# Top-k attention started before the last strip's choice is finished, and the last gate tile of two attentions spread to their ends

## The reference, cut to what matters

```
# fox attention, 16 heads of 64: softmax over causal keys with a forget bias, then a gate
s = einsum(q, k) * scale + (c_q - c_k);  w = softmax(s);  attn = w @ v
y = (attn * silu(g)) @ w_out

# top-k attention, 8 heads of 64: the indexer scores every key, the 128 best are kept
isc = einsum(relu(q_i . k_i), w_i) * idx_scale      # [query, key], causal
_, sel = lax.top_k(isc, 128)                        # ties: lowest key first
p = softmax(q_a . k_a over sel);  oa = p @ v_a

# stick-breaking attention ob, then
merged = sigmoid(gate_a) * (oa @ w_up_a) + sigmoid(gate_b) * (ob @ w_up_b)
```

## Time and profile before

| | |
|---|---|
| median of 3 runs | 1633.67 us (1633.66 to 1635.63) |
| the profiled execution's own time | 1633.67 us |
| span from its first to its last instruction | 1631.9 us |
| mean granted PE clock | 0.993 of 2.4 GHz |
| PE busy | 1554.3 us, 95% of the span |
| DVE busy | 874.0 us, 54% |
| ACT busy | 633.2 us, 39% |
| POOL busy | 609.8 us, 37% |

### The profile page before, as it was taken

One profiled execution on the slowest core, in us unless ns is written; L12 is line 12 of the kernel. 1 busy time (PEld: TensorE's weight loads), 2 busy tenths in 40 slices (PEclk: granted clock), 3 DMA queues, 4 the chain that ended last, 5 costly groups with the idle time before them and its releaser, 6 DMA issues.

```text
span 1631.9 us, 22774 instructions
## 1 busy us (share of the span) xinstructions
PE 1554.3 (95%) x9097; PEld 1204.5 (74%) x9097; DVE 874.0 (54%) x1567; ACT 633.2 (39%) x1140; POOL 609.8 (37%) x452
## 2 busy tenths in 40 slices
PE   7999999999999898999999989989999999999997
PEld 6887666888887666887867766656677877778776
DVE  4895565237881666338069974545576422332224
ACT  5323656254222456353242335644344222212222
POOL 5464112253643212344325422211254344344441
PEclk9999999999999999999999999999999999999999
DMA  9474001152633101242312221101132232322321
GB/s 344 162 277 155 27 28 65 52 206 66 235 100 100 35 28 54 78 142 78 114 55 82 78 80 49 34 26 52 52 142 78 91 103 78 103 90 92 103 78 77
DMA packets 86217, 158.69 MB, mean 97 GB/s; under 512 B 2736, under 2 KB 20704, under 8 KB 86112
## 3 DMA queue, kind: packets, MB, share of 16 engines
q1 hardware_dynamic: 82256, 148.91, 27.1%
q10 hardware_dynamic: 3856, 8.32, 1.5%
HBM read 155.10 MB, written 2.12 MB: 96 GB/s over the span
## 4 chain that ended last, share of the span: by engine, by line
PE 80%; DVE 13%; issue 2%; ACT 2%; POOL 1%; PEld 1%; DMA 1%; DVEq 0%; SPq 0%; PEldq 0%; ACTq 0%
PE banks L403 11%; PE banks L405 10%; PE banks L404 10%; PE banks L399 9%; PE banks L400 8%; PE banks L401 8%; PE banks L521 4%; PE banks L523 3%; PE banks L522 3%; PE banks L546 2%; PE banks L561 2%; PE banks L571 2%; DVE slots L1879 1%; DVE max L1877 1%; PE banks L724 1%
## 5 line engine op out<-in xcount | busy, mean ns | idle before, releaser
L377 POOL TENSOR_TENSOR w_lo<-w_raw,w_hi 128x512 fp32r<-128x512 f32 x440 | 596.3, 1389 | 985.5 <-ACT w_hi L965 985.5
L965 ACT ACTIVATE w_hi<-w_raw 128x2048 fp32r<-128x2048 f32 (+1 forms) x112 | 210.9, 1883 | 209.7 <-DMA w_raw<-w_ff_dram 152.8
L399 PE MATMUL banks<-xh,w_hi 128*128 128x512 f32 x640 | 251.7, 393 | 5.2 <-issue 4.3
L401 PE MATMUL banks<-xh,w_lo 128*128 128x512 f32 x640 | 249.3, 390 | 0.0
L400 PE MATMUL banks<-xl,w_hi 128*128 128x512 f32 x640 | 249.2, 389 | 0.0
L403 PE MATMUL banks<-w_hi,xh 128*128 128x512 f32 x384 | 153.6, 400 | 11.8 <-POOL w_lo L373 9.3
L403 PE MATMUL banks<-w_hi,yh 128*128 128x512 f32 x384 | 152.2, 396 | 8.5 <-issue 4.2
L405 PE MATMUL banks<-w_hi,yl 128*128 128x512 f32 x384 | 150.8, 393 | 0.0
L404 PE MATMUL banks<-w_lo,yh 128*128 128x512 f32 x384 | 150.6, 392 | 0.0
L405 PE MATMUL banks<-w_hi,xl 128*128 128x512 f32 x384 | 150.6, 392 | 0.0
L404 PE MATMUL banks<-w_lo,xh 128*128 128x512 f32 x384 | 150.6, 392 | 0.0
(11 more groups left out here) (326 smaller groups left out, 2504.4 us busy)
## 6 DMA issues: line engine op xcount, KB each, us to landing
w_raw<-w_ff_dram SPq DMA_DIRECT2D x32, 1024.0 KB, 5.2
w_raw<-w_in_dram SPq DMA_DIRECT2D x22, 1024.0 KB, 5.1
work_hi<-w_ada_dram SPq DMA_DIRECT2D x16, 1024.0 KB, 7.1
w_raw<-rec_w_in_dram SPq DMA_DIRECT2D x16, 1024.0 KB, 5.3
w_raw<-att_w_in_dram SPq DMA_DIRECT2D x14, 1024.0 KB, 6.3
work_lo<-w_ada_dram SPq DMA_DIRECT2D x8, 1024.0 KB, 7.5
w_raw<-ple_w_gate_dram SPq DMA_DIRECT2D x8, 1024.0 KB, 5.1
w_raw<-att_w_out_dram SPq DMA_DIRECT2D x4, 1024.0 KB, 5.1
```

Of the source, the lines that this page charges most:

```text
L377: ins = pool.tensor_tensor(wlo[s][:, k, :], raw[s][:, k, :], wh[s][:, k, :].bitcast(F32), ALU.subtract)
L399: pe.matmul(out, w_h, x_h, start=start, stop=False)
L401: return pe.matmul(out, w_l, x_h, start=False, stop=stop)
L965: act.activation(wh[s][:, 0:kn, :], raw[s][:, 0:kn, :], ACT.Copy).then_inc(w_split, 1)
```

## The change

There are three edits.

1. The top attention starts before the third strip's choice is finished. `choose(3)` stops after its 16 rounds. Its first four further instructions (`compare(3)`) are issued by DVE at step 1 of the attention, ahead of that step's score work, the last four (`keep_ties(3)`) at step 3, and the copy for the stick matrices at step 4. Steps 0 to 2 only read strips 0 to 2. `tw` and `eq` move to columns 1024 to 2047 of slot A.
2. The last gate tile of both attentions is spread by `LAST_SPREAD` over six steps in place of four (fox) and four in place of two (top), up to the steps that have no scores any more. ACT empties this tile after its loop and no longer inside it.
3. The waits at the end of PE's `attention` go to where their data is needed. For fox, the wait on the last output is kept for tile 3 of `outa0` alone (bank 6), and the wait for the emptied gate bank follows that group. For top, both waits stand behind the three `stick_first` calls.

```diff
+LAST_SPREAD = {4: [(), (0, 1), (2,), (3,), (4, 5), (6, 7)], 2: [(0,), (1, 2), (3, 4), (5, 6, 7)]}
...
-                    if t < steps:
-                        for k in SPREAD[per][t % per]:
-                            beside(side, t // per, k)
-                pe.wait_ge(sg(x + "_out"), pairs)
-                pe.wait_ge(sg(side + "_free"), KT + 1)
+                    last = t - (steps - per)
+                    for k in SPREAD[per][t % per] if last < 0 else LAST_SPREAD[per][last] if last < per + 2 else ():
+                        beside(side, min(t // per, KT - 1), k)
...
+                       tile_ready=None if l else lambda m: (sg("fox_out"), 8 if m == 3 else 7),
                        between=last_pair_turned if l else None)
+                if l == 0:
+                    pe.wait_ge(sg("g0_free"), KT + 1)
...
             for u in (2, 1, 0):
                 stick_first(0, u)
+            pe.wait_ge(sg("top_out"), 4)
+            pe.wait_ge(sg("ga2_free"), KT + 1)
...
-                    if t % per == 0 and 0 < t <= steps:
+                    if t % per == 0 and 0 < t < steps:
                         emptied(t // per - 1)
...
+                emptied(KT - 1)
+                act.wait_ge(sg(side + "_free"), KT + 1)
...
-            tw, eq = slot["A"][:, 0:512], slot["A"][:, 512:1024]
+            tw, eq = slot["A"][:, 1024:1536], slot["A"][:, 1536:2048]
...
+                if q < 3:
+                    compare(q)
+                    keep_ties(q)
...
-            dve.wait_ge(sg("tri_in"), 16)
-            V.after(dve.tensor_copy(stick[:, :], grow[:, 0:2 * P]))
-            dve.sem_inc(sg("tri_ready"), 1)
-            attention("top", 4, lambda q: isc[...], top_s, output_of_top)
+            def last_strip(step):
+                if step == 1:
+                    compare(3)
+                if step == 3:
+                    keep_ties(3)
+                if step == 4:
+                    dve.wait_ge(sg("tri_in"), 16)
+                    V.after(dve.tensor_copy(stick[:, :], grow[:, 0:2 * P]))
+                    dve.sem_inc(sg("tri_ready"), 1)
+            attention("top", 4, lambda q: isc[...], top_s, output_of_top, last_strip)
```

More of the change, by code:

```diff
@@ L1577, in out_and_ple, with attention @@
                 lows(name, n + TV_T[3], 3)
-            def attention(x, pairs, strip, probs, output):
+            def attention(x, pairs, strip, probs, output, beside=None):
                 steps = 4 * pairs
                 for t in range(steps + 4):
+                    if beside:
+                        beside(t)
                     if t >= 7 and t % 4 == 3:
@@ L1879, in choose, with compare @@
                         V.after(dve.match_replace(w, m8[:, :], w, NEG))
+                if q < 3:
+                    compare(q)
+                    keep_ties(q)
+            def compare(q):
+                kw = (q + 1) * P
+                strip, w, e = isc[:, KOFF[q]:KOFF[q] + kw], tw[:, 0:kw], eq[:, 0:kw]
                 V.after(dve.tensor_scalar(e, strip, m8[:, 7:8], None, ALU.is_equal))
@@ L1883, in choose, with keep_ties @@
                 V.after(dve.tensor_scalar(stat[:, 25:26], stat[:, 24:25], -1.0, float(TOPK), ALU.mult, ALU.add))
+            def keep_ties(q):
+                kw = (q + 1) * P
+                strip, w, e = isc[:, KOFF[q]:KOFF[q] + kw], tw[:, 0:kw], eq[:, 0:kw]
                 V.after(dve.tensor_tensor_scan(strip, e, e, 0.0, ALU.add, ALU.bypass))
@@ L1898, in _ @@
             dve.wait_ge(*emptied(BASE["merge2"][0] - 1))
-            dve.wait_ge(sg("tri_in"), 16)
-            V.after(dve.tensor_copy(stick[:, :], grow[:, 0:2 * P]))
-            dve.sem_inc(sg("tri_ready"), 1)
-            attention("top", 4, lambda q: isc[:, KOFF[q]:KOFF[q] + (q + 1) * P], top_s, output_of_top)
+            def last_strip(step):
[7 more added lines that the diff above has]
+                    dve.sem_inc(sg("tri_ready"), 1)
+            attention("top", 4, lambda q: isc[:, KOFF[q]:KOFF[q] + (q + 1) * P], top_s, output_of_top, last_strip)
             dve.sem_inc(sg("gb2_free"), 1)
```

## The result

The changed kernel takes 1625.58 us (median of 4 runs, 1624.46 to 1627.23), and the kernel before takes 1634.1 us beside it (median of 4, 1633.66 to 1635.63). The ratio is 0.9947, with a 95% interval of 0.993 to 0.9964: faster by about 8.5 us, where 5.9 us were forecast. The direction was forecast right; the time lies 0.4 us under the lower end of the range (1626.0) and 2.2 us under the value named. With the experiments the same kernel ran 15 times: median 1626.28 us, mean 1626.7 us, 1624.46 to 1630.85. The kernel before ran 55 more times beside them (median 1634.15 us, mean 1634.1 us), and once more at 3082.61 us, a run that is left out of all comparisons. By these larger numbers the change is worth 7.3 us by the means and 7.9 us by the medians.

A forecast was written before the change was run, and what follows sets the result against it. PE was taken as the bound, four fifths of the chain, with waits for DVE and a falling clock. Against 1633.67 us: -7.1 (top's start) - 0.4 (fox) + 0.4 (ACT) + 1.2 (clock) = -5.9, so 1627.8 us; range 1626.0 to 1630.8.

The forecast's parts named there:

- The start of top: Start of top attention: PE's 3.6 us wait and 3.5 us of slow clock both go, -7.1 us (-6.7 to -7.3).
- of slow clock: Steps 2 and 3 of top: 3.5 us lost beside the wait, because the clock fell to 1.2 GHz.
- Rival (d): Steps 2 to 4 of top: DVE late, wait only cut, clock still falls; 1631.3 us, chance 0.10.
- Fox: End of fox: PE waits 1.5 to 2 us before step 32, none before `outa0`; gain 0.4 us, between none and 1.
- ACT's chain: End of top: ACT's last gate copy, table load and sigmoids come 0.4 us later, range 0 to 0.7 us.
- the same pieces in the new order: End of top: adding PE's pieces reordered puts the last unit's start at 1040.6, ACT's copy 0.43 us later.
- The clock in stick: Start of stick: the clock falls behind a 3.4 us PE wait, costing 1.2 us, bounds 0 and 3.5.
- (c): Stick: the clock's fall costs as much as the one at 964 us, 3.5 us; 1630.1 us, chance 0.12.
- (e): Stick: the clock, once down, stays down, making the kernel slower than before; 30 us give 1642 us, chance 0.04.
- rival (b): Stick: the clock holds behind the new wait; 1626.6 us, chance 0.24.

The follow-up runs named there:

- the kernel with the filler: The kernel before plus fourteen useless matmuls ahead of the wait that starts top's step 2: 1631.71 us, ratio 0.9992 to the kernel before.
- fox alone: The kernel before with the spread and the moved waits (edits 2 and 3) for fox only, top as before: 1633.72 us, ratio 0.9994.
- the changed kernel's third: The changed kernel, unchanged, run a third time for its runs and a profile: 1626.43 us, ratio 0.9957 to the kernel before.
- top alone: The kernel before with the spread and the moved waits for the end of top only, old start of top: 1634.43 us, ratio 1.0004.
- 36.62 us with the clock held: The changed kernel plus twelve useless matmuls in the wait ahead of gb2's second tile: 1626.12 us, ratio 0.9953 to the kernel before.
- edit 1 alone: The changed kernel with LAST_SPREAD and the moved waits undone, leaving only the new start of top: 1627.66 us, ratio 0.9954 to the kernel before.
- the changed kernel again: The changed kernel, unchanged, run once more for its runs and a second profile: 1626.28 us, ratio 0.9952 to the kernel before.

## Why the prediction was right or wrong

**The start of top: right, and slightly too small.** -7.1 us was forecast and -7.34 us measured, 0.04 us beyond its bounds of -6.7 to -7.3. PE had no wait there, and steps 2 and 3 took 9.14 us for the 9.3 forecast. The reason given for one half was too simple: the 3.5 us "of slow clock" were 2.6 us of clock and about 1.1 us that stay with the clock held, 0.7 of them small waits behind the long one, which the kernel with the filler separates. Rival (d), that DVE would come late, is out: the longer first part was paid by the shorter second.

**Fox: mechanism right, size wrong.** One wait ahead of step 32 was forecast, 1.5 to 2 us, and none before `outa0`; it is 1.58 us, and none. The gain of 0.4 us (its own figures, 280.8 in place of 281.13, give 0.3) is 0.82 us when the clock holds. Part A starts 258.81 - 258.63 = 0.18 us later than before, so on the clock of before PE goes on at 273.09 - 0.18 = 272.91, where 273.2 were forecast, 0.3 us more; and the rows from there to `outa0` take 280.49 - 273.09 = 7.40 us where 7.6 were forecast, 0.2 us more. Those two make the difference. What the prediction did not have is that the clock can fall behind this wait, too. It did in 2 of the 10 profiles of kernels with fox's edit (fox alone, and the changed kernel's third), for 1.5 us each, which is 0.3 us in the mean: by this estimate the edit is worth some 0.5 us, too little for the whole runs to show. The old end of fox is not free of falls either: top alone, which has it, shows one from 282 us on, behind the waits of 1.19 and 0.92 us.

**ACT's chain: wrong sign.** The copy of the last tile was put 0.4 us later; counted from top's 15th score product the table load comes at 1033.31 - 1018.74 = 14.57 us, and at 1041.26 - 1026.53 = 14.73 us before. It came 0.16 us earlier. The step at fault is the last unit's start, "the same pieces in the new order": at 1040.6 it stands 14.07 us behind the score product. ACT's copy, which follows 0.43 us later, came at 1032.70 - 1018.74 = 13.96 us, so the unit started at 13.5 us, 0.54 us earlier than forecast. A row of before shows what the reading behind it left out. The prediction says that PE had next to no wait up to 1041 us; but PE stood still for the last 0.7 us of that:

```profile
1041.30 1.09 PE L571 MATMUL banks<-work_hi,slots 128*64 128x128 f32 x16 [0.99 <-ACT work_hi L1144]
```

The work ahead of this row ended at 1041.30 - 0.99 = 1040.31, and not at 1041. The pieces of the sum are not itemised in the prediction, so it is likely and not shown that this wait is the error. The spread pays 0.16 us and no more, as C = 36.62 us with the clock held shows.

**The clock in stick: right in its mean, wrong as a fixed term.** A wait of 3.4 us with a fall behind it was forecast, and is 3.07 us with a fall behind it. Its cost was taken as 1.2 us: against the 36.62 us with the clock held, the four profiles of the changed kernel cost 1.48, 2.63, 0.03 and 1.18 us, 1.3 in the mean. In the windows of the table 3.4, 5.2, 1.7 and 3.4 us of full-speed work are missing, so some 2 us of each did not reach part C. A large part of this slack can be seen: with the clock held, PE still waits 1.45 us for DVE ahead of the 512-column score product, and in the four profiles it waits 0.33, 0, 0.63 and 0 us there. The prediction put the slack at 1.5 us at most. In the third profile 0.56 us of the fall lay in the long wait itself, from 1044.45 us on, while PE went on at 1045.01. Rivals (c) and (e) did not come; the clock is back at 1.00 each time.

**Why the median lies below the range: the step that failed.** By the profiled execution the sum is -7.34 - 0.82 - 0.16 + 1.48 and 0.2 elsewhere, -6.6 us, and its own time of 1627.23 us is inside the range. Two things put the median under it. First, rival (b), in which the clock holds in stick, was set at 1626.6 us; with the measured terms it is 1633.67 - 7.34 - 0.82 - 0.16 = 1625.3 us, and the lower end of the range was made from the same mis-sized terms. All three errors have one sign: 0.24 + 0.42 + 0.56 = 1.2 us. This is the step that failed: ACT's chain was put at +0.4 us and measured -0.16, fox at -0.4 and measured -0.82, the start of top at -7.1 and measured -7.34, and the range's lower end was not carried to the sum of the low ends (-7.3 - 1.0 + 0 + 0 gives 1625.4, which would have held the 1625.58 us measured). The path and the waits were right; the sizes were off. Second, the mis-sized terms are not all of it: with the measured ones and 1.3 us for the clock the sum is 1626.7 us, still 1.1 us over the median of the four runs, and the range had no term for the median of a few runs. The 55 runs of the kernel before reach from 1630.0 to 1638.05 us, and they go with the clock: mean time 1636.0 us in the 8 runs with a mean granted clock of 0.992, 1634.4 in the 18 with 0.994, 1633.2 in the 15 with 0.995 and 1631.4 in the 6 with 0.996, about 1.1 us for each thousandth. A thousandth of 1632 us is 1.6 us of full-speed work, or about one short fall, as at 1245 us with 5 x 0.34 = 1.7 us missing. The 2.0 us that three runs showed was not the width of this scatter. Over fifteen runs the changed kernel's median is 1626.28 us, just inside the range, so that the four runs fell outside it is in part chance.

That falls of the clock make most of this scatter is shown in place, for parts A and C by the profiles of the changed kernel, and for the stretch to top by all fourteen profiles; for the kernel before it rests on this relation alone. Why a fall comes in one execution and not in the next at the same wait stays open. That the edit at the end of top costs the change about 1.2 us is shown in the profiles; over whole runs the difference of 0.65 us is inconclusive.

## What to carry to other kernels

Work that only the fourth step needs should not stand in front of the first: here 7 us came from a list order alone, and a third of it was the clock that fell behind the wait. Spreading an unrelated product over an engine's last waits pays next to nothing when another engine's chain (here ACT's table loads and sigmoids) sets the end; find that chain and shorten it first. When a wait is made out of several small ones, price the case in which the clock falls behind it and the case in which it does not, and carry each end of every term to the end of the range.

## What the runs showed of the hardware that was not expected

- The same wait of 1.58 us was followed by the lower clock in some executions (0.58 in fox alone, 0.72 over six microseconds in the changed kernel's third profile) and not in the other eight profiles that have it, with the same instructions around it. It is not the shortest: edit 1 alone has a granted clock of 0.66 from 542 to 547 us, with waits of 0.82 and 0.94 us that ended at 540.35 and 542.91 us, and in three profiles the clock fell near 156 us with no wait of PE over 0.6 us in the 7 us before. The Trainium skill ("TensorE: Matmul & The Clock Gate", Part 1) has activity release a throttle that is the default; the traces agree that busy stretches go back to 1.00 (the longest fall before the end of the kernel, in top alone and in the changed kernel again, took 10.2 us), and show besides that the same wait can fall either way.
- A fall can cost less than the work it leaves missing: 1.7 us of missing work cost 0.03 us at the start of stick, 3.4 cost 1.2 to 1.5, and 5.2 cost 2.6. The rest went into waits that PE would have had there.
- Useless matmuls ahead of a wait held the clock in all five places tried (3.34 us of them at the start of top, 2.88 us in stick, and at 646, 756 and 1243 us).
- The same DVE instruction of 128x512 took 0.69 and 1.63 us, and another one 0.49 and 1.18 us, by its place in the two traces.
- A switch of ACT's table showed 1.28 us and the next instruction started 0.01 us behind it (1034.54 + 1.28, and 1035.83).
